# The closing products of a recurrence unit, taken kind by kind over four tiles, with fewer filler products and new begin times

## The chip, the core and the metric

The kernel runs on one core of one Trainium2 chip. The metric is the device time of one execution in microseconds: the median of three runs of the kernel before is 2409.43 us (2409.38 to 2409.88).

## What is computed

Two models of two layers each run one after the other over 256 tokens of width 1024, all in float32. The first model's layer is a gated feed-forward, a mixer with three branches, and a second feed-forward. The second model's layer is a feed-forward, a mixer (sliding-window attention, an mLSTM and an RWKV-7 recurrence), a second feed-forward and a gated embedding. The change touches the RWKV-7 recurrence:

```python
def step(state, xs):
    r_t, w_t, k_t, v_t, a_t, b_t = xs
    sa = jnp.einsum('bhvk,bhk->bhv', state, a_t)
    state = (state * w_t[:, :, None, :] + sa[..., None] * b_t[:, :, None, :]
             + v_t[..., None] * k_t[:, :, None, :])
    return state, jnp.einsum('bhvk,bhk->bhv', state, r_t)
```

It has 4 heads of width 64 and 256 steps, and stands in both layers of the second model.

## The kernel before, in words

All weights come as one stream of 748 pieces (512 KB for most) over SyncE's DMA queue into four slots (`raw`). ScalarE rounds a piece to fp32r (`whi`, L483), VectorE takes the rest (`wlo`, L490), and TensorE makes each product of a gemm as three fp32r products, high by high, low by high, high by low (`gemm`, L509). These are 128x512 products for the most part.

Each engine is one in-order instruction stream. It is written out beforehand: every step is a lane, a generator that yields a begin time before it issues its instructions, and `by_beat` merges the lanes of an engine by these times. `timed` takes the begin times from the table `PLAN`, one row for each lane at each boundary of two parts ("ffn1_2>mix2" holds the whole second mixer). The times set only the order on an engine, which at run time goes by semaphores alone.

`WARM` is a second table. At some begin times of the lanes `pe_norm`, `pe_scores2` and `pe_values2` the function `rewarm` (L498) issues so many 128x512 products of a constant into a bank that is free. Nobody reads them; they are fillers. There are 77 of them: 27 in each of the two second mixers, 23 at other boundaries.

The recurrence is done in chunks of 64 steps. A unit is two chunks: unit 0 holds tokens 0 to 127, unit 1 the others, and tokens of a chunk lie on one half of the 128 partitions (q). `pe_unit` builds for each head and chunk the inverse of a unit triangular 64x64 matrix with plain float32 products on 64x64 tiles of the array, then `XU` (L2180), which ScalarE copies to `xu` (L2237). The closing block (L2200 to L2205) follows: for each of two head groups c, two chunks q and two heads m2 six products of 64x64 by 64x64, 48 in all. The row half of the array is given by q, the column half by m2, so each (q, m2) is one of four tiles of 64x64, and row half q writes bank 2 + q. A float32 product shows in the trace as two passes, each with its weight load. Behind the block, VectorE (L2279 to L2290) makes the transition `Ac`, the input `Ee`, and the rows that `pe_state` and `dve_state` carry from chunk to chunk (L2307, L2313, L2324, L2328).

Around it, on the same engines, stand the projections (gemms), the rotation of the attention's columns `qk` (L995 to L999), their transposes (L516 on `qk`), and eight softmax jobs: scores (L2428), mask and maximum (L2486 to L2491), exponential (L2465), transposes of `S` (L516), copy `PT` (L2474), values (L2453). The mLSTM's products are L2552 to L2582; those that broadcast its rows are L2563. Lines of the parts' boundaries are the transposes of `xs` (L516), `ahi` (L636) and `alo` (L655), which close one part's result into the next part's input.

Of the kernel before, what the change touches and what calls it, by code (L numbers as in the profile page):

```python
# [88 lines left out]
def by_beat(*lanes):  # L89
# [6 lines left out]
    while heads:  # L96
# [5 lines left out]
        else:  # L102
# [8 lines left out]
WARM = {  # L111
    "ffn1_2>mix2": {"pe_norm": (0, 0, 3, 0), "pe_scores2": (0, 0, 0, 0, 0, 2, 0, 5), "pe_values2": (0, 0, 0, 0, 6, 3, 3, 5)},
    "ffn2>ffn1": {"pe_norm": (0, 0, 2, 0)},
    "ffn2_2>ple": {"pe_norm": (0, 0, 0, 2)},
    "final>ffn1_2": {"pe_norm": (0, 3, 3, 0)},
    "mix2>ffn2_2": {"pe_norm": (0, 0, 0, 1)},
    "ple>ffn1_2": {"pe_norm": (3, 6, 0, 0)},
}
# [3 lines left out]
        "act_norm": (9.5, 10.9, 11.82, 27.38),  # L122
        "act_square": (-9.64, -9.3, 14.98, 20.36),
        "dve_norm": (-23.06, -6.14, 25.64, 27.7),
        "dve_square": (9.14, 30.8),
        "pe_norm": (-250.66, -9.66, -9.52, -9.52, -9.46, 4.76, 9.7, 14.5),
        "pool_norm": (6.74, 6.74),
# [214 lines left out]
def program(nc, order, known, dram, out, vecs, consts, misc, bcs, pos, x_in):  # L342
# [1741 lines left out]
    def pe_unit(s, i):  # L2084
# [1008 lines left out]
```

## Time and profile before

| what | value |
|---|---|
| median of three runs | 2409.43 us |
| the profiled execution's own time | 2412.0 us |
| its span, first to last instruction | 2410.7 us |
| mean granted TensorE clock | 0.998 |
| TensorE busy | 2363.4 us, 12525 products |
| VectorE, ScalarE busy | 1515.7 us, 1232.0 us |
| DMA | 166 GB/s mean |

The trace counts both passes of a float32 product, each an instruction. The busy time of TensorE includes the time that a product takes to run through the array, so that a new product can start long before the last one's record ends; how fast products follow one another is read from their starts. The page's rest are waits: a releaser is the instruction whose end let a waiting one go.

### The profile page before, as it was taken

The page shows a single profiled execution, that of the slowest core. Times are in us where ns is not written, and L with a number is a line of the kernel's source. Part 1 is how long each engine was busy: PE and PEld are TensorE (multiplying, and loading weights), DVE is VectorE, ACT ScalarE, POOL GpSimd, SP SyncE. Part 2 cuts the span into 40 slices and gives each one's busy share as a digit, 9 for nine tenths or more (in the row PEclk, how much of TensorE's full clock was granted, in tenths as well). Part 3 has the DMA queues.
Part 4 walks back from the last instruction along what each step waited for, and adds up shares of the span by engine and source line. Part 5 has one row for each costly group of instructions (what it writes and reads, how often), then busy time and mean ns, then how long its engine had stood idle before and what let it go on. Part 6 is the DMA issues. An engine that isn't in the chain of part 4 may idle for free.

```text
span 2410.7 us, 31254 instructions
## 1 busy us (share of the span) xinstructions
PE 2363.4 (98%) x12525; PEld 1933.3 (80%) x12525; DVE 1515.7 (63%) x2297; ACT 1232.0 (51%) x2053; POOL 52.5 (2%) x66
## 2 busy tenths in 40 slices
PE   8999999999999999999999999999999999999998
PEld 6788878888888887888878878778877887877886
DVE  5657786655555678665565577775566557676556
ACT  5446554544544655454454464554455446365445
POOL 0000000000000000000000000010000000000000
PEclk9999999999999999999999999999999999999999
DMA  7554445556565544555555542155555554225563
GB/s 249 182 199 149 135 145 184 177 181 196 170 194 182 164 131 140 181 183 187 185 174 185 194 160 83 45 201 188 188 170 175 183 195 137 83 82 180 183 196 123
DMA packets 110738, 399.95 MB, mean 166 GB/s; under 512 B 12289, under 2 KB 12673, under 8 KB 110337
## 3 DMA queue, kind: packets, MB, share of 16 engines
q1 hardware_dynamic: 110592, 397.96, 50.2%
q8 instruction: 98, 1.61, 0.3%
q14 instruction: 48, 0.39, 0.0%
HBM read 396.86 MB, written 1.05 MB: 165 GB/s over the span
## 4 chain that ended last, share of the span: by engine, by line
PE 92%; DVE 6%; ACT 1%; issue 1%; DMA 0%; POOL 0%; SPq 0%; ACTq 0%; DVEq 0%
PE ps L509 80%; PE ps L516 4%; DVE wlo L490 2%; PE ps L2075 1%; PE ps L1481 1%; PE ps L1445 1%; DVE alo L655 1%; PE ps L498 1%; ACT whi L483 1%; PE ps L2453 0%; PE ps L1436 0%; DVE xs L916 0%; PE ps L2428 0%; ACT ahi L636 0%; DVE up L1929 0%
## 5 line engine op out<-in xcount | busy, mean ns | idle before, releaser
L490 DVE TENSOR_TENSOR wlo<-raw,whi 128x1024 fp32r<-128x1024 f32 (+1 forms) x748 | 893.2, 1211 | 294.4 <-ACT whi L483 288.9
L483 ACT CAST whi<-raw 128x1024 fp32r<-128x1024 f32 (+1 forms) x748 | 764.4, 1040 | 346.3 <-PE ps L509 329.6
L509 PE MATMUL ps<-whi,ahi 128*128 128x512 f32 (+2 forms) x2016 | 798.5, 396 | 17.1 <-DVE wlo L490 12.7
L509 PE MATMUL ps<-wlo,ahi 128*128 128x512 f32 (+2 forms) x2016 | 794.5, 394 | 0.0
L509 PE MATMUL ps<-whi,alo 128*128 128x512 f32 (+2 forms) x2016 | 788.1, 391 | 0.0
L509 PEld LDWEIGHTS ps<-whi,ahi 128*128 128x128 f32 x2016 | 379.9, 188 | 108.8 <-DVE wlo L490 26.1
L509 PEld LDWEIGHTS ps<-whi,alo 128*128 128x128 f32 x2016 | 380.0, 189 | 73.9 <-issue 1.7
L509 PEld LDWEIGHTS ps<-wlo,ahi 128*128 128x128 f32 x2016 | 380.1, 189 | 72.4 <-issue 2.6
L509 PE MATMUL ps<-whi,yhi 128*128 128x512 f32 (+1 forms) x948 | 372.4, 393 | 2.6 <-DVE ylo L837 1.4
L509 PE MATMUL ps<-wlo,yhi 128*128 128x512 f32 (+1 forms) x948 | 370.1, 390 | 0.0
L509 PE MATMUL ps<-whi,ylo 128*128 128x512 f32 (+1 forms) x948 | 369.9, 390 | 0.0
L811 ACT ACTIVATE sil<-ps,stat 128x256 f32<-128x256 f32 x176 | 83.6, 475 | 336.4 <-PE ps L509 326.2
L832 DVE SCALAR_TENSOR_TENSOR hid<-ps,stat,sil 128x256 f32<-128x256 f32 x176 | 85.1, 484 | 270.9 <-ACT sil L811 270.9
L509 PEld LDWEIGHTS ps<-whi,yhi 128*128 128x128 f32 x948 | 178.1, 188 | 41.5 <-DVE wlo L490 4.5
L509 PEld LDWEIGHTS ps<-whi,ylo 128*128 128x128 f32 x948 | 178.0, 188 | 36.4 <-issue 0.7
L509 PEld LDWEIGHTS ps<-wlo,yhi 128*128 128x128 f32 x948 | 178.1, 188 | 35.2 <-issue 0.7
L818 ACT CAST yhi<-ps 128x512 fp32r<-128x512 f32 x88 | 51.6, 586 | 156.9 <-PE ps L516 156.9
L837 DVE TENSOR_TENSOR ylo<-ps,yhi 128x512 fp32r<-128x512 f32 x88 | 60.7, 690 | 108.5 <-ACT yhi L818 108.4
L655 DVE SCALAR_TENSOR_TENSOR alo<-ps,vec,ahi 128x128 fp32r<-128x128 f32 x224 | 61.1, 342 | 19.0 <-ACT ahi L636 19.0
L636 ACT ACTIVATE ahi<-ps,vec 128x128 fp32r<-128x128 f32 x224 | 62.4, 385 | 20.4 <-PE ps L516 20.2
L1498 ACT ACTIVATE S<-S,sm 128x128 f32<-128x128 f32 (+1 forms) x96 | 42.8, 448 | 23.9 <-DVE sm L1529 23.8
L516 PEld LDWEIGHTS ps<-cst,hid 128*128 128x128 f32 x352 | 43.9, 141 | 11.0
(377 smaller groups left out, 1572.8 us busy)
## 6 DMA issues: line engine op xcount, KB each, us to landing
raw<-stream SPq DMA_DIRECT2D x718, 512.0 KB, 4.0
raw<-stream SPq DMA_DIRECT2D x16, 388.0 KB, 3.1
bcb<-bcs SPq DMA_DIRECT2D x9, 512.0 KB, 6.3
raw<-stream SPq DMA_DIRECT2D x8, 416.0 KB, 3.7
raw<-stream SPq DMA_DIRECT2D x4, 384.0 KB, 3.2
cst<-consts SPq DMA_DIRECT2D x1, 1260.0 KB, 7.6
msc<-misc SPq DMA_DIRECT2D x1, 1160.0 KB, 7.5
xs<-xin SPq DMA_DIRECT2D x2, 512.0 KB, 4.4
```

Source lines behind the costliest of these rows:

```text
L483: act.do.copy(whi[:, n % NSP, 0:w], raw[:, n % NRAW, 0:w]).then_inc(*rounded(n))
L490: dve.do.tensor_tensor(wlo[:, n % NSP, 0:w], raw[:, n % NRAW, 0:w], whi[:, n % NSP, 0:w].bitcast(F), ALU.subtract).then_inc(*rest(n))
L498: pe.do.matmul(ps[:, bank, :].rearrange("p (k n) -> p k n", k=4), warm[:, :], warm[:, :].unsqueeze(1).broadcast_to([128, 4, 128]), start=T ...
L509: m = pe.do.matmul(o, a, b, start=(first and q == 0), stop=(last and q == n - 1))
L516: m = pe.do.transpose(o, src, ident)
L636: act.do.mul(ahi[:, c, 128 * i:128 * i + 128], ps[:, 2 * i + hf, 128 * (c % 4):128 * (c % 4) + 128], vc(GAIN[part], l, c)).then_inc(*a_hi( ...
L655: dve.do.scalar_tensor_tensor(alo[:, c, t], ps[:, 2 * i + hf, 128 * (c % 4):128 * (c % 4) + 128], vc(GAIN[part], l, c), ahi[:, c, t].bitca ...
L811: act.do.activation(sil[:, n % 4, :], ps[:, n % 3, 0:256], ACT.Silu, scale=stat[:, 6 + i:7 + i]).then_inc(*silu(s, n))
L818: act.do.copy(yhi[:, y:y + 2, :], ps[:, 3, :].rearrange("p (k t) -> p k t", k=2)).then_inc(*h_hi(s, q))
L832: dve.do.scalar_tensor_tensor(hid[:, n % 4, :], ps[:, n % 3, 256:512], stat[:, 6 + i:7 + i], sil[:, n % 4, :], ALU.mult, ALU.mult).then_in ...
L837: dve.do.tensor_tensor(ylo[:, y:y + 2, :], ps[:, 3, :].rearrange("p (k t) -> p k t", k=2), yhi[:, y:y + 2, :].bitcast(F), ALU.subtract).th ...
L1498: act.do.activation(a[:, q, :], a[:, q, :], ACT.Exp, bias=sm[:, h:h + 1], accum_out=sm[:, z + h:z + h + 1]).then_inc(*job_act(s, n, "exp", q))
```

## The change

The six products of a tile no longer stand in a row. A function `each` issues one kind of product for all four tiles (q, m2) in turn, then the next kind; the operands, the banks and the number of products stay. The filler table `WARM` loses 22 of 77 products: 5 in each second mixer (two ahead of the scores of job 5, two of six ahead of the transposes of job 4, one of five ahead of those of job 7), two at ffn2 to ffn1, two at each of the two ffn2_2 to ple, three at final to ffn1_2, one at each of the two mix2 to ffn2_2, one at ple to ffn1_2. Where no filler stands, the wait for a free bank now stands with the products that write it, not at the earlier begin time. All begin times in `PLAN` are new numbers. The diff, cut to its core (of `PLAN` one line):

```diff
 WARM = {
-    "ffn1_2>mix2": {"pe_norm": (0, 0, 3, 0), "pe_scores2": (0, 0, 0, 0, 0, 2, 0, 5), "pe_values2": (0, 0, 0, 0, 6, 3, 3, 5)},
-    "ffn2>ffn1": {"pe_norm": (0, 0, 2, 0)},
-    "ffn2_2>ple": {"pe_norm": (0, 0, 0, 2)},
-    "final>ffn1_2": {"pe_norm": (0, 3, 3, 0)},
-    "mix2>ffn2_2": {"pe_norm": (0, 0, 0, 1)},
-    "ple>ffn1_2": {"pe_norm": (3, 6, 0, 0)},
+    "ffn1_2>mix2": {"pe_norm": (0, 0, 3, 0), "pe_scores2": (0, 0, 0, 0, 0, 0, 0, 5), "pe_values2": (0, 0, 0, 0, 4, 3, 3, 4)},
+    "final>ffn1_2": {"pe_norm": (0, 3, 0, 0)},
+    "ple>ffn1_2": {"pe_norm": (3, 5, 0, 0)},
 }
...
-        "pe_state": (124.82, 128.16, 130.6),
+        "pe_state": (127.26, 130.52, 133.2),
...
+    def warmth(s, lane, n):
+        counts = WARM.get(boundary(s), {}).get(lane, ())
+        return counts[n] if n < len(counts) else 0
+
     def rewarm(s, lane, n, bank):
 
-        counts = WARM.get(boundary(s), {}).get(lane, ())
-        for _ in range(counts[n] if n < len(counts) else 0):
+        for _ in range(warmth(s, lane, n)):
             pe.wait_ge(warm_dve, "made")
...
                 yield turn_time(s, i, hf) - 0.01
-                wait_banks(s, i, hf)
-                rewarm(s, "pe_norm", 2 * i + hf, 2 * i + hf)
+                if warmth(s, "pe_norm", 2 * i + hf):
+                    wait_banks(s, i, hf)
+                    rewarm(s, "pe_norm", 2 * i + hf, 2 * i + hf)
                 yield turn_time(s, i, hf)
                 wait_x(pe, s, i, hf)
+                wait_banks(s, i, hf)
...
+        tiles = [(slice(64 * q, 64 * q + 64), slice(64 * m2, 64 * m2 + 64), q, m2) for q in range(2) for m2 in range(2)]
         for c in range(2):
-            for q in range(2):
-                r = slice(64 * q, 64 * q + 64)
-                for m2 in range(2):
-                    p, h = slice(64 * m2, 64 * m2 + 64), 2 * m2 + c
-                    X, U, V = xu[i][r, h, 0:64], xu[i][r, h, 64:128], v4[r, m2, c, :]
-                    bt, kt_ = (bkt[i][r, c, 128 * f + 64 * m2:128 * f + 64 * m2 + 64] for f in range(2))
-
-                    def at(o):
-                        return ps[p, 2 + q, o:o + 64]
-                    pe.do.matmul(at(64 * c), X, M(NB)[r, h, :], start=True, stop=True)
-                    pe.do.matmul(at(128 + 64 * c), U, M(NB)[r, h, :], start=True, stop=False)
-                    pe.do.matmul(at(128 + 64 * c), V, M(NK)[r, h, :], start=False, stop=True)
-                    pe.do.matmul(at(256 + 128 * c), X, bt, start=True, stop=True)
-                    pe.do.matmul(at(320 + 128 * c), bt, U, start=True, stop=False)
-                    m = pe.do.matmul(at(320 + 128 * c), kt_, V, start=False, stop=True)
+            def each(o, lhs, rhs, start, stop):
+
+                for r, p, q, m2 in tiles:
+                    m = pe.do.matmul(ps[p, 2 + q, o:o + 64], lhs(r, m2), rhs(r, m2), start=start, stop=stop)
+                return m
...
+            each(64 * c, X, nb, True, True)
+            each(128 + 64 * c, U, nb, True, False)
+            each(128 + 64 * c, V, nk, False, True)
+            each(256 + 128 * c, X, bt, True, True)
+            each(320 + 128 * c, bt, U, True, False)
+            m = each(320 + 128 * c, kt_, V, False, True)
         m.then_inc(*rec_pe(s, i, "out"))
```

TensorE, the second mixer of layer 0, the start of unit 0's closing block. Before (`um` holds the triangular matrices, `bkt` the turned keys):

```order
L509 MATMUL ps<-whi,alo 128x388
L2200 MATMUL ps<-um_129,xu_133 64x64
L2201 MATMUL ps<-um_129,xu_133 64x64
L2202 MATMUL ps<-um_129,Vall 64x64
L2203 MATMUL ps<-bkt_135,xu_133 64x64
L2204 MATMUL ps<-xu_133,bkt_135 64x64
L2205 MATMUL ps<-Vall,bkt_135 64x64
L2200 MATMUL ps<-um_129,xu_133 64x64
L2201 MATMUL ps<-um_129,xu_133 64x64
L2202 MATMUL ps<-um_129,Vall 64x64
L2203 MATMUL ps<-bkt_135,xu_133 64x64
```

And with the change:

```order
L510 MATMUL ps<-wlo,ahi 128x388
L510 MATMUL ps<-whi,alo 128x388
L2198 MATMUL ps<-um_129,xu_133 64x64 x8
L2198 MATMUL ps<-um_129,Vall 64x64 x4
L2198 MATMUL ps<-bkt_135,xu_133 64x64 x4
L2198 MATMUL ps<-xu_133,bkt_135 64x64 x4
L2198 MATMUL ps<-Vall,bkt_135 64x64 x4
L2198 MATMUL ps<-um_129,xu_133 64x64 x8
L2198 MATMUL ps<-um_129,Vall 64x64 x4
L2198 MATMUL ps<-bkt_135,xu_133 64x64 x4
L2198 MATMUL ps<-xu_133,bkt_135 64x64 x4
L2198 MATMUL ps<-Vall,bkt_135 64x64 x4
```

The change's last ten rows are all 48 products of the block. What stands side by side is now the same kind on four tiles (the two kinds with `um` and `xu` print as one row of eight), where six kinds on one tile stood.

TensorE, the same mixer, around job 4's transposes of `S` (lines moved by 1 for L498 to L516 and by 26 to 31 further down). Before:

```order
L509 MATMUL ps<-wlo,ahi 128x512
L509 MATMUL ps<-whi,alo 128x512
L509 MATMUL ps<-whi,ahi 128x512
L509 MATMUL ps<-wlo,ahi 128x512
L509 MATMUL ps<-whi,alo 128x512
L2453 MATMUL ps<-qk_147,PT_153 128x64 x2
L498 MATMUL ps<-warm 128x512 x6
L2552 MATMUL ps<-cst,row 128x4 x4
L516 MATMUL ps<-cst,S_149 128x128 x4
L2428 MATMUL ps<-qkT 128x256 x2
```

With the change:

```order
L510 MATMUL ps<-whi,alo 128x512
L510 MATMUL ps<-whi,ahi 128x512
L510 MATMUL ps<-wlo,ahi 128x512
L2484 MATMUL ps<-qk_147,PT_153 128x64 x2
L510 MATMUL ps<-whi,alo 128x512
L510 MATMUL ps<-whi,ahi 128x512
L510 MATMUL ps<-wlo,ahi 128x512
L510 MATMUL ps<-whi,alo 128x512
L499 MATMUL ps<-warm 128x512 x4
L517 MATMUL ps<-cst,S_149 128x128 x4
L2454 MATMUL ps<-qkT 128x256 x2
```

The fillers are four instead of six and stand behind four more gemm products; the transposes of `S` (job 4) and the scores of job 5 come ahead of the mLSTM's `row` now.

TensorE, the same mixer, the last job. Before:

```order
L2573 MATMUL ps<-cv 128x128
L2453 MATMUL ps<-qk_147,PT_153 128x64 x4
L2563 MATMUL ps<-row,cst 128x256
L498 MATMUL ps<-warm 128x512 x5
L516 MATMUL ps<-cst,S_149 128x128 x4
L2453 MATMUL ps<-qk_147,PT_153 128x64 x4
L2571 MATMUL ps<-cv 128x256
L2573 MATMUL ps<-cv 128x128
L516 MATMUL ps<-cst,o_att 128x128 x8
```

With the change:

```order
L2604 MATMUL ps<-cv 128x128
L2484 MATMUL ps<-qk_147,PT_153 128x64 x4
L499 MATMUL ps<-warm 128x512 x4
L517 MATMUL ps<-cst,S_149 128x128 x4
L2594 MATMUL ps<-row,cst 128x256
L2484 MATMUL ps<-qk_147,PT_153 128x64 x4
L2602 MATMUL ps<-cv 128x256
L2604 MATMUL ps<-cv 128x128
L517 MATMUL ps<-cst,o_att 128x128 x8
```

The broadcast of `row` has moved from ahead of the fillers to the place between the transposes of `S` and the values of job 7, and four fillers stand where five stood.

## Rows read from the trace of the kernel before

**Rows 1.** The page: busy time of TensorE, and the chain that ended last
```profile
PE 2363.4 (98%) x12525; PEld 1933.3 (80%) x12525; DVE 1515.7 (63%) x2297; ACT 1232.0 (51%) x2053; POOL 52.5 (2%) x66
...
PE 92%; DVE 6%; ACT 1%; issue 1%; DMA 0%; POOL 0%; SPq 0%; ACTq 0%; DVEq 0%
```

**Rows 2.** Who waited for whom, TensorE: us in total, times, longest us
```profile
PE ps L509 <- DVE wlo L490: 12.7, 12, 3.2
PE ps L516 <- DVE xs L916: 7.8, 7, 2.1
```

**Rows 3.** Timeline of TensorE, block of unit 0: start us, us, what
```profile
1506.36 0.33 PE L2200 MATMUL ps<-um,xu 64*64 64x64 f32 x2
1506.52 0.28 PE L2201 MATMUL ps<-um,xu 64*64 64x64 f32 x2
1506.64 0.28 PE L2202 MATMUL ps<-um,Vall 64*64 64x64 f32 x2
...
1506.87 0.22 PE L2204 MATMUL ps<-xu,bkt 64*64 64x64 f32 x1
1506.88 0.27 PE L2200 MATMUL ps<-um,xu 64*64 64x64 f32 x1
1506.93 0.22 PE L2204 MATMUL ps<-xu,bkt 64*64 64x64 f32 x1
...
1510.63 0.28 PE L2205 MATMUL ps<-Vall,bkt 64*64 64x64 f32 x2
1510.84 1.09 PE L516 MATMUL ps<-cst,qk 128*128 128x128 f32 x8
```

**Rows 4.** Timeline of TensorE, the eight products of L2129
```profile
1465.40 0.46 PE L2129 MATMUL ps<-B__120,AR 64*64 64x64 f32 x16
1465.80 0.66 PE L1978 MATMUL ps<-cst,up 128*128 128x128 f32 x4
```

**Rows 5.** Timeline of VectorE, last rotation ahead of the transposes of 1510.84
```profile
1507.94 0.33 DVE L999 TENSOR_TENSOR qk<-rtmp 128x160 f32<-128x160 f32 x1
```

**Rows 6.** Timeline of VectorE behind the block of unit 1; idle before in brackets
```profile
1525.27 0.42 DVE L2279 TENSOR_TENSOR Ac<-ps,cst 128x256 f32<-128x256 f32 x1 [6.95 <-PE ps L2205]
```

**Rows 7.** Windows: us, busy of PE, PEld, DVE, ACT, POOL, then PEclk, DMA
```profile
1520.67:1525.16 4.49, 4.49 (x98) 4.42 (x97) 0.00 (x0) 1.11 (x5) 0.00 (x0) 1.00 0.00 0
1535.00:1560.00 25.00, 24.16 (x128) 17.23 (x128) 20.84 (x44) 21.55 (x45) 0.00 (x0) 1.00 0.00 1
...
1229.00:1234.00 5.00, 4.07 (x13) 3.27 (x14) 5.00 (x12) 5.00 (x16) 0.16 (x1) 0.66 0.50 127
```

**Rows 8.** Timeline of TensorE, the filler at the boundary mix2 to ffn2_2
```profile
1593.81 0.40 PE L498 MATMUL ps<-warm 128*128 128x512 f32 x1
1594.04 0.60 PE L516 MATMUL ps<-cst,xs 128*128 128x128 f32 x4
```

**Rows 9.** Timeline of TensorE, the filler ahead of job 4
```profile
1540.22 1.66 PE L498 MATMUL ps<-warm 128*128 128x512 f32 x6
1541.81 0.41 PE L2552 MATMUL ps<-cst,row 4*128 4x4 f32 x4
```

**Rows 10.** Timeline of ScalarE, the last exponentials of jobs 4 and 7
```profile
1541.16 0.18 ACT L2465 ACTIVATION_READ_ACCUMULATOR S<-S,sm 128x1 f32 x1
...
1555.85 0.19 ACT L2465 ACTIVATION_READ_ACCUMULATOR S<-S,sm 128x1 f32 x1
```

**Rows 11.** Timeline of TensorE at the end of job 7
```profile
1555.65 0.69 PE L2563 MATMUL ps<-row,cst 4*128 4x256 f32 x2
1556.28 1.42 PE L498 MATMUL ps<-warm 128*128 128x512 f32 x5
1557.54 0.60 PE L516 MATMUL ps<-cst,S 128*128 128x128 f32 x4
1558.81 1.10 PE L2453 MATMUL ps<-qk,PT 128*128 128x64 f32 x8 [0.68 <-ACT PT L2474]
```

**Rows 12.** Timeline of TensorE behind the filler of final to ffn1_2
```profile
1229.93 0.77 PE L509 MATMUL ps<-whi,ahi 128*128 128x512 f32 x1 [1.20 <-DVE alo L655]
```

More of the change, by code:

```diff
@@ L121 @@
     ">ffn1": {
[L122 to L127, printed above, removed]
+        "act_norm": (4.82, 12.8, 15.66, 29.18),
+        "act_square": (-12.6, 4.8, 15.84, 19.8),
+        "dve_norm": (-12.06, -8.24, 24.98, 25.76),
+        "dve_square": (25.44, 34.48),
@@ new lines @@
+        "act_norm": (19.98, 21.7, 23.88, 26.3),
+        "act_pool1": (108.04, 117.98, 119.24, 123.72),
+        "act_project1": (47.96, 59.82, 83.44, 102.76),
+        "act_square": (17.9, 25.68, 25.68, 25.9),
+        "act_sums1": (151.54, 185.22),
+        "act_turn1": (111.44, 118.08, 188.9, 190.16),
+        "act_turns1": (63.78, 78.3, 102.76),
+        "dve_add": (11.66, 11.66, 20.04, 21.86),
[8 rows of a table added]
+        "dve_latent": (30.72, 35.34, 35.34, 35.36, 36.18, 37.4, 38.12, 43.44, 43.44, 49.54, 49.54, 49.54, 49.68,
+            49.68, 49.68),
@@ new lines @@
+        "dve_norm": (13.82, 21.96, 27.46, 30.9),
+        "dve_post": (9.86, 9.86, 9.94, 17.1, 19.02, 20.6),
+        "dve_project2": (29.2, 34.44, 35.96, 36.14, 36.94, 36.94, 45.9, 49.88, 49.88, 49.88, 52.62, 60.98, 84.74,
+            149.86, 159.44),
+        "dve_rope2": (111.12, 111.44, 112.14, 124.68),
+        "dve_square": (25.94, 25.94),
+        "dve_state": (130.02, 139.6, 144.58),
+        "dve_sums2": (155.26, 158, 173.56, 173.7),
+        "dve_turn2": (175.08, 176.92),
+        "dve_unit0": (53.4, 54.04, 67.76, 80.88, 88.6, 96.84, 109.94, 120.74),
@@ L267 @@
[L267 to L274 removed]
+        "act_norm": (12.64, 16.06, 22.26, 22.58),
@@ L317 @@
-        "pool_norm": (30.7, 30.7),
-        "pool_post": (-18.08, -0.38),
+        "act_norm": (19.08, 20.66, 20.98, 20.98),
+        "act_post": (6.04, 7.72, 15.74, 19.3),
+        "act_square": (19.18, 19.48, 21.96, 25.04),
+        "dve_norm": (18.04, 19.64, 21.64, 24.68),
+        "dve_post": (10.26, 10.26, 14.62, 15.9, 18.28, 18.58),
+        "dve_square": (19.62, 26.04),
+        "pe_norm": (3.7, 3.7, 11.54, 11.54, 19.4, 22.02, 22.88, 24.86),
+        "pool_norm": (35.34, 35.76),
+        "pool_post": (-22.86, 14.54),
@@ L2435, in pe_values2, with bank_free @@
             k = 128 * (i + 1)
-            if n:
-                pe.wait_ge(job_act, s, n - 1, "back")
-            else:
-                pe.wait_ge(lstm_dve, s, "mq")
-            rewarm(s, "pe_values2", n, 7)
+            def bank_free():
+                if n:
+                    pe.wait_ge(job_act, s, n - 1, "back")
+                else:
+                    pe.wait_ge(lstm_dve, s, "mq")
+            if warmth(s, "pe_values2", n):
+                bank_free()
+                rewarm(s, "pe_values2", n, 7)
             yield org(s) + 20 + t + 3.0
             pe.wait_ge(job_act, s, n, "exp", 1)
+            bank_free()
             m = turns(*((ps[:, 7, 128 * q:128 * q + 128], S2[:, n % 2, 128 * q:128 * q + 128])
```

280 lines of the change are left out of this document (136 added, 144 removed), and 61 rows, old and new, of the table PLAN.

## The prediction

> **What bounds the kernel now.** I read the page first. TensorE is busy for 98% of the span and holds 92% of the chain that ended last [rows 1]. The next question is how much of its time is waiting. The view of who waited for whom names two waits that count: 12.7 us for the low halves of weights and 7.8 us for the residual at boundaries [rows 2]. So a product that is made shorter gives its time to the whole, unless the engine then reaches a wait. The timeline shows which products are slow for what they do, and the windows show what the other engines do meanwhile.
>
> **The closing block.** Unit 0's block starts at 1506.36 and what follows it starts at 1510.84 [rows 3]: 4.48 us for 48 products, 96 passes. A product in the middle of its tile's row of six has 0.12 us (1506.52 to 1506.64), so a pass is 0.058 us: a weight load and the product on the same tile follow each other. The next tile's first product starts at 1506.88, ahead of the second pass of L2204 on the tile before (1506.93). So tiles do overlap, but only at the seams, for the last three passes of twelve.
>
> The trace has a block in the order that the change gives. L2129 goes round the same four tiles, and each row half writes a bank of its own there too: eight products, 16 passes, from 1465.40 to the next instruction at 1465.80 [rows 4], 0.40 us. At two tiles at a time 16 passes would need 8 x 0.058 = 0.46 us and their start-up; at four they need 4 x 0.058 = 0.23 us and 0.17 us for the first load and the way to the next instruction. So it is four. The changed block then takes 96/4 = 24 rounds: 24 x 0.058 + 0.17 = 1.56 us. It saves 4.48 - 1.56 = 2.92 us, and the four blocks (two units, two layers) save **11.7 us**. Bounds from the same rows: nothing less than 0.40 us for 16 passes has been seen, and 6 x 0.40 = 2.40 us would be the block if each sixteen passes paid the start anew, a saving of 8.3 us in all. I take 11.7, since start-up falls away in a row of 96.
>
> Does it arrive? Behind unit 1's block it does. From 1520.67 to 1525.16 VectorE does nothing at all [rows 7], and it idles 6.95 us until the block ends [rows 6]. Its work then starts 2.9 us earlier, and with it the softmax jobs and the group norm. Behind unit 0's block stand the transposes of `qk`, which need the rotation that ends at 1507.94 + 0.33 = 1508.27 [rows 5]. The block would end at 1506.36 + 1.56 = 1507.92. So 0.35 us there turns into a wait, twice: **0.7 us given back**. What is late next is VectorE's rotation, not the block.
>
> **The fillers.** One costs 0.23 us where work stands behind it (1593.81 to 1594.04) [rows 8]. 22 of them are 5.1 us at most. By place:
> - Eight at ffn2 to ffn1, ffn2_2 to ple and mix2 to ffn2_2 stand as that one does, with a ready transpose behind: 8 x 0.23 = 1.8 us.
> - Three at final to ffn1_2 stood ahead of a wait of 1.20 us for `alo` [rows 12]. That wait grows by what they leave: 0. The one at ple to ffn1_2 I also count at 0, its 0.23 us goes to the range.
> - Job 4: the exponential ends at 1541.16 + 0.18 = 1541.34 [rows 10], the six fillers and what follows let the next product start at 1541.81 [rows 9]. Two fillers less give about 0.4 us a layer: 0.8 us. The two ahead of job 5's scores I count at 0: in 1535 to 1560 VectorE is busy for 20.84 of 25 us and ScalarE for 21.55 [rows 7], so that stretch is theirs, and TensorE would wait in place of filling.
> - Job 7: its exponential is done at 1555.85 + 0.19 = 1556.04 [rows 10], before the five fillers begin at 1556.28 [rows 11]. They only delay the transposes. Also `row`'s broadcast (1555.65 to 1556.28, 0.63 us) moves into the place where TensorE waited 0.68 us for the copy [rows 11]. That is 0.23 + 0.63 = 0.86 us a layer: 1.7 us.
>
> Together 4.3 us.
>
> **The begin times.** They move gemm products between the steps and change no amount of work. The wait for a bank that moved behind its early begin time is still ahead of the same products, and nothing new queues behind it. The new numbers can win at most the two waits named, 20.5 us [rows 2], and would need every one of these 19 waits to go; they can lose too. I take 0, with 3 us either way in the range. DMA, the POOL and the SP rows keep their order.
>
> **Sum.** -11.7 + 0.7 - 4.3 = -15.3 us. The profiled execution takes 2412.0 us and would take 2396.7. The median of the runs is 2.6 us below the profiled one, so the forecast is **2394.1 us**, 0.6% faster. About 0.2%, 4.8 us, is what a measurement of this kernel tells from no change.
>
> **Rivals.**
> - *Only two tiles at a time.* In the block consecutive products share a row half, in L2129 a column half. If weight loads within a row half took turns, a round of four would last two: 48 x 0.058 + 0.17 = 2.95 us, a saving of 1.53 x 4 = 6.1 us, and the time 2409.4 - 6.1 - 3.6 = 2399.7 us. Against it: L2129's 16 passes hold pairs with the same row half too, and 0.40 us leaves no room for turns. The Trainium skill ("TensorE: Matmul & The Clock Gate", The mechanism) states that weight loads overlap running products only when the row group differs, and that products start strictly in program order. By that rule the time would be this rival's; the trace disagrees, with 1506.88 ahead of 1506.93 in rows 3 and 0.40 us in rows 4.
> - *Every product pays for coming to a new tile: slower.* The first product on a tile takes 0.16 us to the next (1506.36 to 1506.52) against 0.12 in a row [rows 3]. If the change of tile broke the overlap, all 48 would pay it: 48 x 0.165 = 7.9 us for a block, 3.4 us more than 4.48, times four 13.8 us; less 3.6 for fillers it is 2419.6 us. It decides from 0.094 us a product on, where the block is as long as before. Against it stands rows 4, 0.05 us a product.
> - *The block is shorter, but the mixer's end is not earlier.* The softmax jobs with their exponentials, at 21.55 of 25 us on ScalarE [rows 7], would then set the end, and fewer fillers only show the wait. Each block's gain is lost, 11.7 us, and 2409.4 - 3.6 = 2405.8 us remain, inside 0.2%. Against it: that work itself starts behind unit 1's block [rows 6].
> - *The clock.* Fillers stand where TensorE idles. In 1229 to 1234 the granted clock was 0.66 [rows 7], that is the lower level of 1.2 GHz for part of the time, behind a wait of 1.20 us [rows 12] and the idle time before it: 5 x 0.34 = 1.7 us lost. If the thinner filling brings four more such stretches, 6.8 us, the time is 2400.9 us.
>
> **How the numbers follow.** Forecast 0.70, two tiles 0.09, slower by tile changes 0.04, end not earlier 0.09, clock 0.08. Downward the range takes the 3 us of the begin times and the eight fillers counted at 0 (three, one and twice two, 8 x 0.23 = 1.8 us): 2394.1 - 4.8 = 2389.3, rounded to 2389. Upward it reaches past the two-tile and the clock case (2399.7 and 2400.9) to 2402. What is left out, the third and second rivals and some of the tails, is 2 in 10. Faster by over 0.2% are the forecast, the two-tile and the clock case, and a third of the one where only part arrives: 0.90. Within 0.2% lie 0.06, slower 0.04.
>
> **What would show it.** The block of unit 0 lasts 1.5 to 1.6 us to its next instruction, with four starts close together and then 0.058 us of pause. 2.9 us would be the two-tile rival, 7.9 the slow one. VectorE's idle time ahead of L2279 falls from 6.95 to about 4 us. The transposes of `qk` show a short wait for VectorE. Fillers number 55. In the feed-forward parts nothing changes. The third rival shows in a mixer whose length from unit 1's block to the transposes of `o_att` grew by the 2.9 us; the clock in windows below 1.00 at the boundaries. The forecast is wrong if waits of TensorE for `wlo` or `xs` grow by more than 5 us.

## The result, and the profile after

| | before | changed |
|---|---|---|
| median of the runs beside each other | 2412.14 us (20 runs, 2409.38 to 2416.44) | 2402.64 us (20 runs, 2399.04 to 2417.0) |
| ratio | | 0.9968, 95% interval 0.9959 to 0.9977 |
| profiled execution, its span | 2412.0 us, 2410.7 us | 2403.77 us, 2402.5 us |
| mean granted TensorE clock | 0.998 | 0.996 |

The kernel is 0.3% faster. Forecast were 0.6% and 2394.1 us, with a range that ended at 2402: the measured time lies just outside it. Between the medians lie 9.5 us and between the two profiled spans 8.2, where 15.3 were forecast. A third of the miss of 8.5 us is the base: the forecast started from the median of three runs, 2409.43 us, and the 20 runs of the same kernel have 2412.14, 2.7 us more. From that base the forecast would have been 2396.8, and a range as wide would have held the measured time. A few executions ran longer at a lower mean clock and none of them is a profiled one: three of the changed kernel (2416.0 to 2417.0 us at 0.989 to 0.990) and, of the kernels in the experiments below, two of e2 (2419.9 and 2420.8), one of e6 (2414.9), and one each of e3 and e4 (3358.5 and 4409.8, left out of the ratios).

The page of the changed kernel, where [rows 1] stood before:
```profile
PE 2351.7 (98%) x12503; PEld 1919.8 (80%) x12503; DVE 1515.8 (63%) x2297; ACT 1233.8 (51%) x2053; POOL 52.1 (2%) x66
...
PE 90%; DVE 6%; ACT 3%; issue 1%; POOL 0%; DMA 0%; SPq 0%; ACTq 0%; DVEq 0%
```
TensorE still bounds the kernel. Its busy time fell by 11.7 us, yet the span by only 8.2. Who waited for whom (total us, times, longest us), against [rows 2]:
```profile
PE ps L510 <- DVE wlo L488: 13.6, 12, 3.2
PE ps L517 <- DVE xs L919: 8.0, 7, 2.2
```
Both waits grew by less than 1 us, far from the 5 us that the prediction had named as a sign of being wrong. The timeline of TensorE at the block of unit 0 (start us, us, what), against [rows 3]:
```profile
1505.81 0.46 PE L2198 MATMUL ps<-um,xu 64*64 64x64 f32 x16
...
1507.14 0.30 PE L2198 MATMUL ps<-Vall,bkt 64*64 64x64 f32 x8
1507.76 0.87 PE L517 MATMUL ps<-cst,qk 128*128 128x128 f32 x6 [0.32 <-DVE qk L1002]
```
The products follow one another four at a time. From 1505.81 to the start of the transposes at 1507.76 is 1.95 us, of which 0.32 is the wait for the rotation. Unit 1's block takes 1.56 us. VectorE behind that block (idle before in brackets), against [rows 6]:
```profile
1517.36 0.42 DVE L2517 SCALAR_TENSOR_TENSOR S<-ps,cst 128x256 f32<-128x256 f32 x1 [1.43 <-PE ps L2454]
...
1519.37 0.43 DVE L2300 TENSOR_TENSOR Ac<-ps,cst 128x256 f32<-128x256 f32 x1 [0.94 <-PE ps L2198]
```
The windows of the changed kernel (us, busy of PE, PEld, DVE, ACT, POOL, then PEclk and DMA), where [rows 7] had one at 0.66:
```profile
1228.00:1233.00 5.00, 4.13 (x13) 3.14 (x14) 5.00 (x12) 4.89 (x15) 2.12 (x1) 0.66 0.53 165
1542.00:1547.00 5.00, 5.00 (x23) 3.86 (x21) 3.83 (x6) 2.78 (x9) 0.00 (x0) 0.66 0.00 0
1815.00:1820.00 5.00, 4.89 (x18) 3.72 (x17) 4.56 (x10) 1.67 (x7) 1.03 (x2) 0.66 0.51 156
2006.00:2011.00 5.00, 3.78 (x14) 3.39 (x15) 5.00 (x9) 5.00 (x15) 0.00 (x0) 0.66 0.47 161
2129.00:2134.00 5.00, 5.00 (x22) 3.77 (x20) 3.92 (x6) 2.78 (x8) 0.00 (x0) 0.66 0.00 0
```
This is where a part of the gain went. In five places the granted clock is at its lower level (0.5, that is 1.2 GHz in place of 2.4) for 3.41 us. Before, there were two, at 1229.9 and 2011.5. The three new ones are at 1542.9 and 2130.0, behind job 4 of each second mixer, and at 1816.0, behind ple to ffn1_2.

To see what they cost I cut the trace at products that every kernel has, and took the time from one to the next. The table is worked out from starts of the timelines. "Tail" is from the end of unit 1's block to the start of the fifth of the eight transposes of `o_att` (the last one follows 0.33 us later where the clock is up). "First model's mixer" is from one set of transposes of `hid` to the next around that mixer (190.9 to 447.9 in the kernel before), "ple" the same around the part ple (1765.6 to 1835.0), with the boundaries ffn2_2 to ple and ple to ffn1_2 inside, and "front" from such transposes (1995.0) into the second mixer. An asterisk marks a stretch at half clock inside. The columns e1 to e12 are the kernels of the next section, by the number that their names begin with; e9 is the changed kernel once more.

| us | before | changed | again (e9) | e1 | e2 | e3 | e4 | e5 | e6 | e10 | e12 |
|---|---|---|---|---|---|---|---|---|---|---|---|
| first model's mixer, layer 1 | 257.00 | 256.49 | 256.48 | 256.96 | 256.91 | 256.46 | 256.51 | 256.47 | 256.37 | 256.55 | 256.43 |
| block, unit 0 | 4.48 | 1.95 | 1.96 | 1.96 | 4.48 | 4.48 | 1.95 | 1.95 | 1.96 | 1.96 | 1.95 |
| block, unit 1 | 4.48 | 1.56 | 1.56 | 1.56 | 4.49 | 4.49 | 1.56 | 1.56 | 1.56 | 1.56 | 1.56 |
| tail, layer 1 | 36.10 | 36.94* | 36.93* | 36.11 | 35.89 | 35.36 | 35.65 | 35.36 | 35.63 | 35.66 | 40.72* |
| tail, layer 2 | 36.11 | 36.93* | 38.53* | 36.12 | 35.88 | 35.35 | 35.62 | 35.36 | 35.65 | 35.66 | 42.27* |
| ple | 69.33 | 70.30* | 69.33 | 69.34 | 69.62* | 70.27* | 69.29 | 70.12* | 69.31 | 70.09* | 69.97* |
| front, layer 2 | 30.85* | 30.88* | 31.16* | 30.84* | 30.84* | 30.89* | 29.73 | 29.79 | 29.70 | 29.70 | 29.70 |

In a tail one stretch costs 36.94 - 35.36 = 1.58 us, against e5, which has two fillers more there and no stretch (e3, with the fillers of the changed kernel and none either, has the same 35.36). The one behind ple to ffn1_2 costs 70.30 - 69.33 = 0.97 us, two executions of one and the same kernel; in other kernels a stretch there costs 0.29 us (e2) to 0.94 (e3). The three new ones make 2 x 1.58 + 0.97 = 4.1 us.

### The profile page after: what moved, and what is told of

It reads as the page before. It is cut to its first block, busy times and chain, and to the rows that moved or that the text cites. A ratio compares the mean times of both kernels' runs of the same rounds, so it can differ in the third digit from the quotient of the medians.

```text
span 2402.5 us, 31221 instructions
## 1 busy us (share of the span) xinstructions
PE 2351.7 (98%) x12503; PEld 1919.8 (80%) x12503; DVE 1515.8 (63%) x2297; ACT 1233.8 (51%) x2053; POOL 52.1 (2%) x66
## 4 chain that ended last, share of the span: by engine, by line
PE 90%; DVE 6%; ACT 3%; issue 1%; POOL 0%; DMA 0%; SPq 0%; ACTq 0%; DVEq 0%
PE ps L510 80%; PE ps L517 4%; DVE wlo L488 2%; PE ps L2078 1%; PE ps L1484 1%; PE ps L1448 1%; DVE alo L658 1%; ACT whi L481 1%; DVE xs L919 1%; PE ps L1439 0%; PE ps L2484 0%; ACT ahi L639 0%; DVE tm L2048 0%; PE ps L499 0%; PE ps L2602 0%
## 5 line engine op out<-in xcount | busy, mean ns | idle before, releaser
L517 PE MATMUL ps<-cst,xs 128*128 128x128 f32 x224 | 37.0, 295 | 16.3 <-DVE xs L919 8.0
```

Of the source, the lines that this page charges most:

```text
L517: m = pe.do.transpose(o, src, ident)
```

## The experiments

All times in this part are medians beside runs of the kernel before on the same chip (2411.93 us beside e1 to e4, 2411.66 beside e5 to e8, 2410.49 beside e9 to e12). Between sets the kernel before thus differs by over 1 us, and small differences between kernels of different sets mean nothing. What is read from a timeline comes from one execution of each kernel.

**First set: the parts alone.** The first kernel (e1) has the new order in the block and everything else as before.
```diff
-                    pe.do.matmul(at(64 * c), X, M(NB)[r, h, :], start=True, stop=True)
-                    pe.do.matmul(at(128 + 64 * c), U, M(NB)[r, h, :], start=True, stop=False)
...
+            each(64 * c, X, nb, True, True)
+            each(128 + 64 * c, U, nb, True, False)
```


> The kernel before with the new order of the closing block alone (old fillers, old begin times). The block is the whole gain (theory A, from the two traces: four blocks shorter by 2.53 and 2.93 us): 10 to 11 us less than before, ratio 0.9957, two stretches at half clock as before. If the gain needs the new begin times (rival B), since the old ones leave the engine waiting behind the shorter block, it is 3 to 8 us, and waits of TensorE grow in the second mixers.

Measured: 2402.87 us against 2411.93, ratio 0.9962 (0.9950 to 0.9974). That is 9.1 us less, a little short of theory A's 10 to 11; the profiled execution, the fastest of the five (2400.29 us), has a span 11.7 us shorter than the kernel before. The blocks are at 1.96 and 1.56 us, the tails at 36.11 as before. What comes behind the blocks keeps its length: the gain arrives at the end, and TensorE was the bound there. The way from unit 0's block to unit 1's grew by 0.3 us (9.83 to 10.13). The five runs lie between 2400.3 and 2404.7 us, and the slower three have a mean clock of 0.995 to 0.997, the two fast ones 0.998. So with all 77 fillers in place the clock was lost in some executions of this kernel too.

The second (e2) has the new filler table alone.
```diff
-    "ffn1_2>mix2": {"pe_norm": (0, 0, 3, 0), "pe_scores2": (0, 0, 0, 0, 0, 2, 0, 5), "pe_values2": (0, 0, 0, 0, 6, 3, 3, 5)},
-    "ffn2>ffn1": {"pe_norm": (0, 0, 2, 0)},
...
+    "ffn1_2>mix2": {"pe_norm": (0, 0, 3, 0), "pe_scores2": (0, 0, 0, 0, 0, 0, 0, 5), "pe_values2": (0, 0, 0, 0, 4, 3, 3, 4)},
```


> The kernel before with the 22 fillers taken away and nothing else. My prediction's term: 4.3 us less. Theory A (fillers stand where TensorE would wait, and keep its clock): no gain, 0 to 2 us more, with one to four stretches more at half clock than the two of before. Rival C (fillers cost nothing either way): within 0.5 us, clock as before.

Measured: 2411.28 us, ratio 1.0003 (0.9993 to 1.0013). 22 fillers less gave nothing that can be measured, where the prediction's term was 4.3 us; the one more stretch at half clock is theory A's, the time within 1 us is nearly rival C's. TensorE's timeline at ffn2 to ffn1 shows why; first the kernel before:
```profile
619.86 0.62 PE L498 MATMUL ps<-warm 128*128 128x512 f32 x2
620.32 0.40 PE L509 MATMUL ps<-whi,ylo 128*128 128x512 f32 x1
620.55 0.60 PE L516 MATMUL ps<-cst,xs 128*128 128x128 f32 x4
...
621.91 0.47 PE L509 MATMUL ps<-whi,ahi 128*128 128x512 f32 x1
```
and the same place with the new table:
```profile
620.24 0.60 PE L513 MATMUL ps<-cst,xs 128*128 128x128 f32 x4
...
622.06 0.48 PE L506 MATMUL ps<-whi,ahi 128*128 128x512 f32 x1 [0.52 <-DVE alo L652]
```
The transposes come 0.31 us earlier, but the product behind them needs `alo` from VectorE, and waits 0.52 us for it. Before, there was no wait. The tails gained 0.2 us each, all of it at job 7 (one filler of 0.23 us less), and a new stretch at half clock stood at 1820.7.

The third (e3) is the changed kernel with the old block, the fourth (e4) the changed kernel with the old filler table:
```diff
-            each(64 * c, X, nb, True, True)
...
+                    pe.do.matmul(at(64 * c), X, M(NB)[r, h, :], start=True, stop=True)
```
```diff
-    "final>ffn1_2": {"pe_norm": (0, 3, 0, 0)},
-    "ple>ffn1_2": {"pe_norm": (3, 5, 0, 0)},
...
+    "final>ffn1_2": {"pe_norm": (0, 3, 3, 0)},
+    "ple>ffn1_2": {"pe_norm": (3, 6, 0, 0)},
```


> The changed kernel with the old order of the closing block: new begin times, fewer fillers, blocks of 4.48 us. Theory A with clock losses: 1 to 3 us more than before. If begin times alone give back (rival D): the same 1 to 3 us more, but with the clock as before. By my prediction it would be 4.3 us less than before.

> The changed kernel with the 77 fillers of before. Theory A: the clock stays up where the fillers are back, two or three half-clock stretches instead of five, and it is 1 to 3 us faster than the changed kernel, 10 to 12 us less than before. By my prediction it would be 4.3 us slower than the changed kernel. If begin times are what gave back (rival D): the same as the changed kernel within 0.5 us.

Measured: with the old block 2410.73 us, ratio 0.9995 (0.9986 to 1.0004), no gain, where theory A had 1 to 3 us more than before and the prediction 4.3 less. With the old fillers 2399.53 us, ratio 0.9949 (0.9936 to 0.9962), which is 3.1 us less than the changed kernel (0.9959 to 0.9977; the intervals just touch). So there is no gain without the new order of the block, and taking the fillers out, with the new begin times, cost some of it. Tails at 35.36 (old block, new fillers), 35.65 (new block, old fillers) and 36.94 us (both new) can't be a sum of work: thinner filling saves 0.3 us, and the combination loses 1.58 to the clock. The fourth kernel has one stretch at half clock, at 1229.8, where the changed one has five.

e1 and e4 differ by the begin times (and, where no filler stands, by the place of the wait for a bank): both have the new block and the old fillers. All four comparable runs of e4 (2399.1 to 2399.9 us, mean clock 0.998) are faster than all five of e1 (2400.3 to 2404.7), 3.3 us by the medians. Their profiles don't show it, with spans of 2398.6 and 2399.0 us, since e1's is that of its fastest execution. So the new begin times help the short block to its full gain, most likely by the clock too; where e1 loses it in its slower executions no profile shows.

**Second set: the clock, place by place.** Job 4's two fillers back in the changed kernel (e5); all others back but those two (e6); all back and six more at final to ffn1_2 (e7). The first pair of lines is against the changed kernel, the other two against e4, which has all of them back:
```diff
-"pe_values2": (0, 0, 0, 0, 4, 3, 3, 4)
+"pe_values2": (0, 0, 0, 0, 6, 3, 3, 4)
...
-"pe_values2": (0, 0, 0, 0, 6, 3, 3, 5)
+"pe_values2": (0, 0, 0, 0, 4, 3, 3, 5)
...
-"final>ffn1_2": {"pe_norm": (0, 3, 3, 0)}
+"final>ffn1_2": {"pe_norm": (0, 3, 9, 0)}
```


> The changed kernel with two fillers put back ahead of job 4's products in each second mixer (four in all), nothing else. Theory A (the clock): the changed kernel's half-clock stretches at 1542.9 and 2130.0 come from the thinned filling there behind the shorter block. With the fillers back both stretches are gone, the stretch from unit 1's block to the transposes of o_att falls from 36.94 and 36.93 to 35.5 to 35.7 us, and the median falls by 2.5 to 3 us against the changed kernel's 2402.6, to about 2400. Theory B (the tail grew by the new order of its jobs, not by the clock): four fillers of 0.23 us add up to 0.9 us, the tails grow to 37.2 to 37.4, the median is 2402.6 to 2403.5.

> The changed kernel with all the fillers of before except the two ahead of job 4's products in each second mixer. Theory A (the clock, place by place): the stretches at 1542.9 and 2130.0 stay, with tails of 36.9 to 37.2 us, while those at 1816.0 and 2007.2 are gone (ple part 69.3 instead of 70.3 us); against the same kernel with every filler of before (2399.5) it is 2.5 us slower, about 2402. Theory B (the two fillers of job 4 are 0.4 us of work a layer and no more): 2398.8, 0.8 below 2399.5, and no stretch at those two places. Theory C (the other fillers near the tail, ahead of job 5 and job 7, hold the clock too): as theory B, with the tails at 35.2.

> The changed kernel with all the fillers of before, and six more at final to ffn1_2 (3 to 9 ahead of the second half's transposes), where TensorE waits 1.41 us for xs anyway at 1229.53. Theory A (the clock): the one half-clock stretch left, at 1229.8, goes; its cost is 0.7 to 1.7 us, so the median is 2397.8 to 2398.8 against 2399.5. Theory B (fillers there only delay): six times 0.23 us is 1.4 us, of which what is over the wait arrives: 2399.5 to 2400.2, and the stretch stays.

Measured: 2400.62, 2401.39 and 2399.09 us; ratios 0.9953 (0.9941 to 0.9966), 0.9962 (0.9951 to 0.9973), 0.9950 (0.9939 to 0.9962).

The first (e5) went as theory A said, with both stretches gone and a gain at the lower end: four fillers more make the kernel 2.0 us faster, where 2.5 to 3 were expected. The windows ahead of the fall and in it, of the changed kernel:
```profile
1537.00:1543.00 6.00, 5.42 (x30) 3.50 (x29) 5.77 (x8) 5.93 (x10) 0.00 (x0) 1.00 0.00 1
1543.00:1546.00 3.00, 3.00 (x11) 2.27 (x11) 2.83 (x6) 0.79 (x4) 0.00 (x0) 0.50 0.00 0
```
and the same windows of e5:
```profile
1537.00:1543.00 6.00, 5.67 (x32) 3.63 (x31) 5.29 (x13) 5.92 (x9) 0.00 (x0) 1.00 0.01 1
1543.00:1546.00 3.00, 3.00 (x19) 2.30 (x19) 2.93 (x4) 2.02 (x6) 0.00 (x0) 1.00 0.00 0
```
TensorE was busy for 5.42 of 6 us ahead of the fall and for 5.67 where it did not fall. Then 3 us hold 11 products in the one and 19 in the other.

In the second (e6) the profile went against theory A. With job 4 thin and the others back, neither tail has a stretch (35.63 and 35.65 us), so theory C holds for that execution: either pair of fillers was enough. But that was one of its fastest executions (2398.27 us). Ten of its 11 runs lie between 2398.2 and 2404.9 us, where the fourth kernel's four comparable ones lie between 2399.1 and 2399.9. So these two fillers seem to matter in some executions, and what one profile shows at one place is not the rule for the kernel. It shows also what two fillers at job 4 are worth without the clock: nothing (tails of 35.65 us in e4 and 35.63 in e6). TensorE in the kernel with six of them (e4):
```profile
1535.99 1.53 PE L502 MATMUL ps<-warm 128*128 128x512 f32 x6
...
1541.75 0.70 PE L2605 MATMUL ps<-cv 64*128 64x256 f32 x2
```
and with four (e6):
```profile
1534.08 1.08 PE L502 MATMUL ps<-warm 128*128 128x512 f32 x4
...
1539.83 0.70 PE L2605 MATMUL ps<-cv 64*128 64x256 f32 x2 [0.27 <-ACT cv L2638]
```
They take 5.76 and 5.75 us from the first filler to the product on `cv`. With fewer fillers a wait for ScalarE stands there. ScalarE's timeline of the changed kernel, which has that wait too (0.26 us at 1540.70), tells what it does:
```profile
1536.15 1.28 ACT L1901 ACT_TABLE_LOAD   x1
1537.44 0.84 ACT L1901 ACTIVATE og<-ps,stat 128x256 f32<-128x256 f32 x2
1538.30 1.28 ACT L2635 ACT_TABLE_LOAD   x1
1539.59 1.06 ACT L2635 ACTIVATE cv<-cv 128x1024 f32<-128x1024 f32 x1
```
Two changes of its function table, 1.28 us each, stand on the path to `cv`.

The third (e7) has no stretch at half clock but those at start and end, as theory A said. Its median is the lowest of all, but 0.3 us over the 2397.8 to 2398.8 of theory A and only 0.4 below e4's. It proves little by itself: e1 and e6 had no stretch at 1229 either, with the fillers of the kernel before at that place.

**Third set: chance, plenty and none.** The changed kernel once more (e9); with all fillers of before and, inside waits for `xs`, 8 more in each second mixer and 6 at two other boundaries (e10); and without any (e12):
```diff
+    "ffn1_2>mix2": {"pe_norm": (0, 0, 11, 0), "pe_scores2": (0, 0, 0, 0, 0, 2, 0, 5), "pe_values2": (0, 0, 0, 0, 6, 3, 3, 5)},
...
+    "final>ffn1_2": {"pe_norm": (0, 3, 9, 0)},
...
+    "ple>ffn1_2": {"pe_norm": (9, 6, 0, 0)},
...
 WARM = {
-    "ffn1_2>mix2": {"pe_norm": (0, 0, 3, 0), "pe_scores2": (0, 0, 0, 0, 0, 0, 0, 5), "pe_values2": (0, 0, 0, 0, 4, 3, 3, 4)},
-    "final>ffn1_2": {"pe_norm": (0, 3, 0, 0)},
-    "ple>ffn1_2": {"pe_norm": (3, 5, 0, 0)},
 }
```


> The changed kernel once more, unaltered, beside the others of this set. Theory A (a half-clock stretch falls on a place or misses it by chance, the same in every kernel with this filling): the profile shows another set of stretches than 1228.9, 1542.9, 1816.0, 2007.2 and 2130.0, and the runs spread over 2399 to 2405 us again. Theory B (the filling alone decides): the same five stretches at the same places, and the median 2402.6 with little spread.

> The changed kernel with every filler of before and more of them where TensorE waits over 1.4 us for xs: 3 to 11 at ffn1_2 to mix2 (wait 2.23 us), 3 to 9 ahead of the second half at final to ffn1_2, 3 to 9 ahead of the first at ple to ffn1_2 (wait 1.75 us). Theory A (idle time at a boundary is what brings the stretches, and fillers inside a wait are free): no stretch except at start and end, in most executions; a median of 2398.2 to 2399.0, the spread under 2 us. Theory B (fillers delay what stands behind them): 2400 to 2402, with TensorE ready later than xs at these places.

> The changed kernel without one filler at boundaries, scores and values (55 fewer). Theory A (fillers hold the clock): more half-clock stretches, at least eight in the profile, each 0.7 to 1.7 us; the median 2404 to 2412. Theory B (fillers are work and no more; what they free arrives): 55 x 0.23 us less waits, up to 6 us below the changed kernel, 2397 to 2402.

Measured: 2402.73, 2399.60 and 2422.79 us; ratios 0.9962 (0.9949 to 0.9976), 0.9953 (0.9941 to 0.9966) and 1.0045 (1.0032 to 1.0057).

The same kernel again has other stretches: none behind ple to ffn1_2, and a double one, 6.83 us, in layer 2's tail. The windows there:
```profile
1815.00:1820.00 5.00, 4.60 (x20) 3.33 (x21) 4.56 (x10) 2.19 (x9) 1.48 (x2) 1.00 0.52 156
...
2129.00:2138.00 9.00, 9.00 (x37) 7.04 (x36) 6.42 (x13) 4.03 (x13) 0.00 (x0) 0.62 0.00 0
```
That tail has 38.53 us, 3.17 over 35.36, twice the 1.58 of one stretch. Both profiles of this filling have stretches in both tails, and no profile of a kernel with all four blocks short and more filling has (e1, e4, e5, e6, e7, e10). At the boundaries it is partly chance.

With plenty the five runs lie within 1.8 us (2398.9 to 2400.7), as theory A expected, against 6.6 us for the five of the changed kernel beside it. The median is 0.6 us over theory A's 2399.0 and not lower than e4's. One stretch is left, at 1813.2, behind a wait of 2.18 us for `alo`. At the boundaries all places of the filler table lie ahead of transposes, and none in that wait.

Without fillers the time is 20 us over the changed kernel, far more than theory A's 2412, and not through many short stretches as it expected but mainly through two long ones. The windows behind job 4 in layer 1 and 2:
```profile
1542.00:1570.00 28.00, 28.00 (x104) 23.35 (x104) 20.10 (x44) 14.01 (x36) 1.06 (x2) 0.51 0.23 72
...
2133.00:2163.00 30.00, 28.70 (x103) 23.61 (x104) 20.87 (x39) 16.73 (x39) 0.00 (x0) 0.50 0.13 42
```
The clock falls at the same place as in the changed kernel, and stays low for 27 and 31 us: tails of 40.7 and 42.3 us. In the 6 us ahead (1537 to 1543) TensorE was busy for 4.04 us.

**The order of the tiles.** Two kernels, e8 and e11, give each block its own order. In e8, unit 0 takes two tiles in turn that share neither half, unit 1 two that share a row half. The numbers are places in `tiles`: 0 and 1 are the two of row half 0, 2 and 3 those of row half 1, and 0 and 2 share a column half.
```diff
+        groups = {(0, 0): ((0, 3), (1, 2)), (0, 1): ((0, 1), (2, 3)), (1, 0): ((0, 2), (1, 3)), (1, 1): ((0, 3, 1, 2),)}[way]
+        for group in groups:
+            for o, lhs, rhs, start, stop in steps:
+                for k in group:
+                    r, p, q, m2 = tiles[k]
+                    m = pe.do.matmul(ps[p, 2 + q, o:o + 64], lhs(r, m2), rhs(r, m2), start=start, stop=stop)
```


> The changed kernel with each of its four closing blocks in another order. Layer 1's unit 0: two tiles in turn that share neither row half nor column half, then the other two; unit 1: two tiles in turn that share a row half; layer 2's unit 0: two tiles in turn that share a column half; unit 1: all four tiles in turn, each next one in the other row half and mostly the other column half. Theory A (each tile runs by itself, 0.058 us a pass, whatever runs beside it): 48 rounds of 0.058 us and the start, 2.9 to 3.1 us for each of the first three blocks, 1.56 us for the fourth. Theory B (products in the same row half take turns in loading): the pair in one row half takes 96 passes in a row, 5.6 to 5.8 us, the other two pairs 2.9 to 3.1, the fourth 1.56 or less. Theory C (two tiles with the same column half take turns at the output): the third block 5.6 to 5.8 us. Three blocks at 2.95 in place of 1.56 make the kernel 4.2 us slower than the changed one, about 2406.8.

The orders meant for layer 2 did not come about: the selection named only the unit, and both layers ran the first two. Measured: 2403.18 us, ratio 0.9964 (0.9950 to 0.9978), all four blocks 2.77 us (theory A: 2.9 to 3.1). TensorE's timeline of the pair in one row half, unit 1 of layer 2:
```profile
2106.22 0.45 PE L2231 MATMUL ps<-um,xu 64*64 64x64 f32 x8
...
2108.99 0.50 PE L510 MATMUL ps<-whi,alo 128*128 128x512 f32 x1
```
The time is 3.6 us under theory A's 2406.8. The blocks cost 0.82 us more at unit 0 and 1.21 at unit 1, 4.1 in all, close to the 4.2 that theory A had for three slower blocks. But the tails have no stretch at half clock in the profile (35.35 us both, against 36.94), which gives 3.2 back. It is the same filling with a longer block ahead, as in e3, and again no stretch; e11 shows that this is no rule.

In e11 the groups are these, by layer and unit:
```diff
+        groups = {(0, 0): ((0, 2), (1, 3)), (0, 1): ((0, 3, 1, 2),), (1, 0): ((0,), (1,), (2,), (3,)), (1, 1): ((0, 1, 2), (3,))}[way]
```


> The closing blocks in four more orders (the selection by layer in the run before named only the unit, so both layers had its first two orders). Layer 1's unit 0: two tiles in turn that share a column half, then the other two; unit 1: four in turn, diagonal neighbours. Layer 2's unit 0: one tile after the other, twelve products each; unit 1: three tiles in turn, then the fourth. Theory A (0.058 us a pass on a tile, tiles independent, an overlap of three passes at each seam): 2.77, 1.56, 96 x 0.058 less three seams of 3 x 0.058 and the start, 5.1 to 5.3, and 2.77 us. Theory B (same column half takes turns at the output): the first 5.3 to 5.6 us, the second as 1.56 or longer, the fourth 3.5 us or more. With one tile at a time it is about 5 us over the changed kernel, near 2407.

Measured: 2403.16 us, ratio 0.9973 (0.9959 to 0.9988). The pair in one column half takes 2.77 us, four in turn by the diagonal 1.56, one tile after the other 5.20, three and one 2.77. TensorE's timeline of the third:
```profile
2089.28 0.44 PE L2231 MATMUL ps<-um,xu 64*64 64x64 f32 x4
...
2094.49 0.77 PE L517 MATMUL ps<-cst,qk 128*128 128x128 f32 x5
```
The blocks go by theory A of both, at 0.058 us a pass on a tile, whatever stands beside it. 48 rounds of 0.058 are 2.78 us. The time of e11 was expected near 2407, with about 5 us for the slower blocks. They did cost 5.3 us (0.82, 0, 3.25 and 1.21), but the profile has a single stretch at half clock, at 1228.5, and tails of 35.37 us. (Block lengths here and in the table are from first start to next start.) Which halves two tiles share makes no difference to the length.

## Why the prediction was right in part, and where it failed

**The block: right.** Forecast were 1.56 us, 2.92 less, and 0.35 us given back at unit 0. Measured are 1.56 us behind unit 1 and 1.95 with a wait of 0.32 behind unit 0, together 10.9 us where 11.0 were forecast. The first kernel (e1) shows that it arrives: 11.7 us by the spans, 9.1 by the medians, and its slower executions have a lower mean clock. That also rules out the rival of the mixer's end that does not come earlier, as its tails kept their 36.11 us. VectorE's idle time ahead of the group's first step fell further than the 4 us forecast, to 0.94 and 1.43 us, because three of its softmax steps now stand between.

**The tile rivals: wrong, and settled.** Changing tiles with each product costs nothing that a block of 1.56 us would leave room for (that rival had 7.9). A pair that shares a row half takes 2.77 us, the same as one that shares none. The rule that the prediction weighed (the Trainium skill, "TensorE: Matmul & The Clock Gate", The mechanism, by which weight loads overlap products only in another row group) does not hold for these products: by it the pair in one row half would have needed about 5.6 us, an estimate from 96 passes of 0.058 us. These rivals were also priced with 3.6 us for the fillers less the 0.7 us given back at unit 0. That 0.7 exists only where the block is short and its gain arrives; without it the two-tile case is 2399.0 us, not 2399.7, and the slow case and the one of the mixer's end are 0.7 lower too.

**The fillers: the step of the sum that failed.** "Together 4.3 us" was three sizes, and the second kernel shows nothing of it in the time. By place:
- Eight at boundaries "stand as that one does, with a ready transpose behind", 1.8 us. The transposes do come earlier, but at ffn2 to ffn1 the product behind them waits for `alo` (0.52 us in e2), which the prediction had seen at one boundary only. There the piece between two sets of transposes of `hid` kept its length in e2 (28.60 to 28.62 us); with the new begin times the two fillers did cost 0.47 (29.22 us in e4, 28.75 in the changed kernel), but the new times had made that piece 0.6 us longer. The other six gave nothing: the piece that holds mix2 to ffn2_2 has 44.26 us with them (e4) and 44.27 without (changed), the ple part 69.29 (e4) and 69.33 (e9).
- Job 4, 0.8 us: nothing, since ScalarE's `cv` is late next, by 0.27 us (e6). The sum took the nearest product behind the fillers and not the one that waits next. The table loads of 1.28 us were in the trace.
- Job 7, 1.7 us, with the moved broadcast: right. From the first of job 6's values to the first transpose of `o_att` the kernel before needs 6.15 us, e2 5.93 (one filler less, 0.22), e4 5.39 (the broadcast moved, 0.76) and the changed kernel 5.16. That is 0.99 a layer where 0.86 was forecast. The wait of 0.68 us for the copy [rows 11] is gone; the changed kernel has the broadcast in its place:
```profile
1552.45 0.60 PE L517 MATMUL ps<-cst,S 128*128 128x128 f32 x4
1552.97 0.69 PE L2594 MATMUL ps<-row,cst 4*128 4x256 f32 x2
1553.72 1.10 PE L2484 MATMUL ps<-qk,PT 128*128 128x64 f32 x8
```
But the tail ahead of job 6's values grew by about 0.25 a layer (29.46 us before, 29.70 in e3), with the new begin times, so the tails gained 0.74 each without the clock (36.10 to 35.36).

So the tails gave 1.5 us in all, and the eight at boundaries and job 4 next to nothing, in place of 4.3.

**The clock: given 0.08 and left out of the sum.** The rival as priced, four more stretches of 1.7 us, is close to what happened: three more, of 1.58, 1.58 and 0.97 us, 4.1 in all. 15.3 forecast, less 2.8 for the fillers, less 4.1 for the clock, is 8.4; 8.2 were measured by the spans. This account is of two single executions; the medians differ by 9.5 us. The prediction had the fillers as work that delays, and asked only what they cost. The runs show that they also hold the granted clock: taking 22 out beside an old block changes nothing (e2), taking them out beside the short block, with the new begin times, costs 3.1 us (e4), taking all out costs 20 us more (e12), and putting four back at job 4 gives 2.0 us and removes both stretches in the tails (e5). They are not all that holds it: e1 has all 77 with the short block, and a median of 2402.87 us, no better than the changed kernel's. A loss of clock beside the short block should have been in the sum, and its case, with a chance of 0.08, was too cheap.

**Begin times: 0, right for the work, not for the time.** In the profiles the first model's mixers gained 0.5 us each and the tails 0.45 each; ffn2 to ffn1 lost 0.6 us, the front of the second mixer in layer 1 0.3 and the last 54 us of the kernel 0.6. That nothing would change in the feed-forward parts was thus not so. With the old fillers the kernel of new times and the kernel of old times have spans of 2398.6 (e4) and 2399.0 us (e1). By the medians the new times are 3.3 us ahead (2399.53 against 2402.87), a little more than the 3 us that the prediction allowed either way. No run has the new begin times alone, without the new block.

**What stays open.** Why either pair of fillers in a tail is enough in one execution and not in another isn't settled: the executions differ in where stretches fall, and only one or two of each kernel were profiled. e11 has the thin filling and a last block of 1.56 us in layer 1, and no stretch in that tail (35.37 us). A direct comparison of the changed kernel with the better ones on one chip was made for e10 alone (e9 2402.73 against 2399.60 us). The medians of the kernels with all fillers or more (2399.1 to 2399.6) can't be told from one another. They are faster than before by 0.5% and than the changed kernel by about 3 us, and any of them is the better version.

## What to carry to other kernels

Small float32 products on quarter tiles should go round the tiles, one product each, and not stay on one tile: the time falls with the number of tiles in flight (here 5.20 us tile by tile, 2.77 two at a time, 1.56 four at a time). A filler product counts twice, by the time it delays and by the clock it helps to hold. Before taking one out, follow the path to the next wait behind it, and if a wait stands there, leave it. When a change makes TensorE's work shorter, the same idle time weighs more: look at the granted clock at every place where it may fall, compare the spread of the runs and not one profile with one profile, and take more than one profile, since the same kernel shows other stretches from one execution to the next.

## What the runs showed that I had not expected

- Two tiles of 64x64 that share a row half, a column half or neither run in turn at the same rate (2.77 us for 96 passes), three at a time are as fast a round as four (2.77 us for three and one, 24 rounds each).
- Each stretch at half clock in the changed kernel lasts 3.41 us; 6.83 us in e9 and 27.3 and 30.7 us in e12 were the longer ones. The clock falls behind idle time, on work that is dense again (3.00 of 3 us busy from 1543.0 on).
- Without one filler the clock stays low over work in which TensorE is busy all the time: 28.00 of 28 us at 0.51.
- Two kernels that differ in little but the begin times (e1 and e4) have spans within 0.4 us in their profiles, and medians 3.3 us apart.
